# Value products on plain fp32 operands in the last slots of both expert layers

## The chip, the cores and the metric

One Trainium2 chip, one core. The metric is device time in microseconds (us) of one launch. The engines are TensorE (PE, with its weight loads shown as PEld), VectorE (DVE), ScalarE (ACT), GpSimd (POOL) and SyncE (SP), which here only issues transfers. The kernel before takes 2854.83 us, the median of 3 runs (2848.03 to 2857.15).

## The reference

Two trunk layers of a diffusion backbone over 384 tokens (128 context, 256 latent) of width 1024, each a mixer (attention with gated linear attention, then a state-space layer) and an expert layer called PEER. Only the expert layer is touched:

```
def peer_ffn(h, w_query, sub_keys, u_tab, v_tab):
    ...                       # 8 heads, top 16 of 128 x 128 product keys: idx, gates g
    def block(args):
        hx, ix, gx = args
        act = jax.nn.gelu(jnp.einsum('td,tkd->tk', hx, u_tab[ix]))
        return jnp.einsum('tk,tkd->td', gx * act, v_tab[ix])
```

Each of 384 tokens picks 128 of 16,384 experts. An expert is a row of u_tab, whose product with the token goes through gelu and a gate, and a row of v_tab, which is added with that weight. All data are fp32.

## The kernel before, in words

**Dense and fetched tokens.** Most tokens are computed densely, against all experts, in 128 blocks of 128 experts. The first tokens (64 in layer 0, 128 in layer 1) are instead served by fetching their own expert rows: POOL issues an indirect transfer of 128 rows of 4 KB (L2273) into a ring of 3 (layer 0) or 5 (layer 1) buffers, and DVE multiplies or adds one such tile (`fetched`, L2428 to L2449). That leaves 320 dense tokens in layer 0 and 256 in layer 1. Layer 0 has 64 fetched tokens and so 128 tiles, one a slot; layer 1 has 256 tiles, two a slot.

**Slots.** The dense part runs in a ring. A slot z.n (0 to 127) does the value products of block n and the score products of block n + RING, where RING is 36 in layer 0 and 38 in layer 1. In the last 36 slots of layer 0 (from 92) and the last 38 of layer 1 (from 90) there is no score block left; they hold value products alone.

**High and low parts.** A product of fp32 matrices is made of fp32r products: ACT copies a high part rounded to fp32r, DVE subtracts it to get the low part (`lo_part`, L163), and TensorE adds high x high, high x low and low x high.

**One slot without a score block**, engine by engine, each in program order:
- SP (L1966): waits until the low part of value block n is made (`vlow`), then loads value block n + VALUES (512 KB, L1928) into the buffer that block n frees. VALUES is 2 in layer 0 and 4 in layer 1. Behind it in the same queue it loads stored gates (L1932) once `applied` allows: in layer 0 the gates of slot n + 2 in every slot (160 KB), in layer 1 those of four slots in every fourth (384 KB). In layer 0 there follow now and then a modulation row of layer 1 (`mrow`, 512 KB, L1989) and a store of a state-space table (`s_wv`, 512 KB, L1769).
- DVE (L2547): `apply` multiplies the activations of slot n + 1 by their gates (L2489, and L2492 in layer 1); in layer 0 it then does one modulation operation (L2529, slots 6 to 117) and two table builds (L1792 to L1807, slots 8 to 103); then `value_low` and `gated_low`, the low parts of value block and gated activations of slot n + 1 (all at L163); then `fetched` once or twice.
- ACT (L2234): `value_high` (L2216) and `gated_high` (L2222) of slot n + 1.
- TensorE (L2084): waits `vlow` and `wlow`, then runs 16 fp32r matmuls with 512 moving columns in layer 0 (4 of them at L2091 for the folded tile of 64 tokens, 12 at L2097) and 12 in layer 1, and increments `valued`.

All of it is written as one fixed order per engine; only semaphores tie the engines together.

Of the kernel before, what the change touches and what calls it, by code (L numbers as in the profile page):

```python
# [32 lines left out]
P = 128  # L33
# [4 lines left out]
NT = T // P  # L38
# [59 lines left out]
class Stage:  # L98


    def __init__(self, nc, sems, name):
        self.nc, self.sems, self.name, self.mem = nc, sems, name, ExitStack()
# [1561 lines left out]
NB = NKEYS  # L1664
CT = 8
HALF = P // 2
# [17 lines left out]
class Plan:  # L1684
# [3 lines left out]

    def __init__(self, fetched, groups, held, each, values, early):
        self.fetched = self.first = fetched
        self.folded = fetched == HALF
        self.tokens = T - fetched
        self.tiles = range(fetched // P, NT)
        self.chunks, self.parts = self.tokens // CT, self.tokens // HALF
        self.held, self.each, self.values = held, each, values
        self.stored = self.parts - held
        self.odd_stored = (self.parts + 1) // 2 - held
        self.spans = [range(sum(groups[:g]), sum(groups[:g + 1])) for g in range(len(groups))]  # L1700
        assert self.spans[-1].stop == self.chunks
        self.last = GATED + len(groups)
        self.ring = self.last + TAIL
        self.fetches = [[] for _ in range(self.last + NB)]
        n = 2 * fetched
        for i in range(n):
            at = GATED + i * len(groups) // early if i < early else self.last + (i - early) * NB // (n - early)
            self.fetches[at].append(i)
# [3 lines left out]
        return (part + self.parts) % 2  # L1712


PLANS = Plan(64, [3] * 12 + [2] * 2, 0, 1, 2, 0), Plan(128, [2] * 16, 1, 4, 4, 0)


class Slot:
# [8 lines left out]

    def has(self, ahead):
        return self.n + ahead < NB

    def turn(self, ahead):
        return (self.n + ahead) // 2
# [110 lines left out]
def mix_experts(nc, s, cx, d, layer, plan, hi, lo, acc, total, ahead):  # L1843
# [75 lines left out]
    with nc.Block() as block:  # L1919
        @block.sync  # L1920
        def _(sp):
            def table(block, b):
                src = d["peer_u"][layer, bass.ds(block, 1)]
                sp.dma_start(ur[:, b], src.rearrange("a p (k m) -> p (a k) m", k=KC)).then_inc(uload[b], 16)

            def value(n):
                src = d["peer_v"][layer, bass.ds(n, 1)]
                sp.dma_start(loaded_value(n), src.rearrange("a p m -> p (a m)")).then_inc(vload[n % VALUES], 16)  # L1928

            def gate(m):  # L1930
                src = gates_dram[0:plan.stored, :, m * EACH:(m + 1) * EACH, :]
                sp.dma_start(gr[:, m % 2], src.rearrange("h p a c -> p h (a c)")).then_inc(gload[m % 2], 16)  # L1932

            sp.dma_start(keys[:], d["sub_keys"][layer]).then_inc(keys_loaded, 16)
            for b in range(2):
                sp.sem_inc(uload[b], 16)
            with sp.Fori(1, J // 2) as i:
                for b in range(2):
                    sp.wait_ge(ulow, i * 4 + 2 * b + 2)
                    src = d["w_query"][layer, bass.ds(i * 2 + b, 1)]  # L1940
                    sp.dma_start(ur[:, b], src.rearrange("a p k m -> p (a k) m")).then_inc(uload[b], 16)
            sp.wait_ge(nm.ready, KC)
            sp.dma_start(d["x_kept"], cx.x[:]).then_inc(xkept, 16)
            with sp.Fori(0, (LOW + 2) // 2) as i:
                for b in range(2):
                    sp.wait_ge(ulow, i * 4 + 2 * (J + b) + 2)
                    table(i * 2 + b, b)
            for n in range(LOW + 2, RING + 2):
                if n == RING - 2:
                    sp.wait_ge(gst0, 16 * PIECES * (PARTS // 2))  # L1950
                    value(0)
                    value(1)
                if n == RING:
                    sp.wait_ge(gst1, 16 * plan.odd_stored)
                    if plan.held:
                        sp.wait_ge(gst2, 16 * (PIECES - 1) * plan.odd_stored)
                    gate(0)
                    gate(1)
                sp.wait_ge(ulow2, n - 2 - LOW + 1)
                table(n, n % 2)  # L1960
            sp.wait_ge(gated, CHUNKS)
            for n in range(2, VALUES):
                value(n)
            sp.dma_start(cx.x[:], d["x_kept"]).then_inc(xback, 16)

            def slot(z):  # L1966
                b = z.n % 2
                if z.has(VALUES):
                    sp.wait_ge(vlow, z.n + 3)
                    value(z.n + VALUES)  # L1970
                if z.has(RING + 2):
                    sp.wait_ge(ulow2, z.n + (RING - LOW + 1))
                    table(z.n + (RING + 2), b)
                if z.has(2):
                    if (z.n + 1) % EACH == 0 and z.n + 1 + EACH < NB:
                        sp.wait_ge(applied, z.n + 1)
                        if z.n + 2 >= SOON and not plan.held:
                            sp.wait_ge(gst2, 16 * ((PIECES - 1) * (plan.odd_stored - 1) + 2))
                        gate((z.n + 1) // EACH + 1)
                if layer == 0:  # L1980
                    if z.n == ROWS_FROM - ROWS_AHEAD:
                        sp.wait_ge(gst2, 16 * ((PIECES - 1) * ((PARTS + 1) // 2 - 1) + 2))
                        sp.dma_start(silu[:], d["silu"]).then_inc(silu_loaded, 16)
                        sp.dma_start(bias[:], d["ada_b"].rearrange("p l j -> p (l j)")[:, 2 * MODS - LATE_MODS:]).then_inc(late_loaded, 16)
                        sp.dma_start(normg[:], d["norm_g"][:, 2:4]).then_inc(late_loaded, 16)
                    for row in (r for r in range(LATE_MODS) if row_slot(r) - ROWS_AHEAD == z.n):
                        if row >= ROWS_AHEAD:
                            sp.wait_ge(row_used, row - ROWS_AHEAD + 1)
                        sp.dma_start(mrow[:, row % ROWS_AHEAD], d["ada_rows"][IN_ROWS + OUT_ROWS + row]).then_inc(row_loaded[row % ROWS_AHEAD], 16)  # L1989
                    builds.transfers(sp, z.n)  # L1990

            for n in range(NB):
                slot(Slot(plan, n))
            sp.wait_ge(xback, 16)
            if layer == 0:
                sp.wait_ge(builds.stored, 16 * Builds.UNITS)

        @block.tensor
        def _(pe):
# [83 lines left out]

            def slot(z):  # L2084
                b = z.n % 2
                pe.wait_ge(vlow, z.n + 3)
                pe.wait_ge(wlow, z.n + 1)
                if plan.folded:
                    for rhs in (vh, vl):
                        for c in range(2):  # L2090
                            pe.matmul(acc[:, c, :], r32(pair[:, b, 0:P]), r32(rhs[:, b, c * 512:(c + 1) * 512]),  # L2091
                                      start=False, stop=False, skip_group_check=True)
                for t in range((FROM + HALF) // P, NT):
                    w = slice(t * P - FROM, (t + 1) * P - FROM)
                    for lhs, rhs in ((wh, vh), (wh, vl), (wl, vh)):
                        for c in range(2):
                            mm = pe.matmul(acc[:, 2 * t + c, :], r32(lhs[:, b, w]), r32(rhs[:, b, c * 512:(c + 1) * 512]),  # L2097
                                           start=False, stop=False, skip_group_check=True)
                mm.then_inc(valued, 1)
                if z.has(RING):  # L2100
                    product(z.n + (J + RING), b, ulow2, z.n + (RING - LOW + 1), whole=True)
# [5 lines left out]
        def _(act):  # L2107
# [126 lines left out]
            def slot(z):  # L2234
                b = z.n % 2
                if z.has(RING - 1):
                    if z.n:
                        act.wait_ge(wlow, z.n)
                    gelu(z.n + (J + RING - 1), 1 - b, z.place(-1))
                if z.has(1):  # L2240
                    value_high(z, 1)
                    gated_high(z, 1)
                if z.has(RING + 1):
                    high(z.n + (J + RING + 1), 1 - b, z.turn(J + RING + 1), uhigh2)
                expert_gelu(LAST + z.n)
                if z.n == 0 and not plan.held:
                    store_rest(PARTS - 1, SOON + REST, NKEYS)
# [29 lines left out]
        def _(dve):  # L2277
# [269 lines left out]
            def slot(z):  # L2547
                if z.has(1):
# [6 lines left out]
                            modulated()  # L2555
                    if layer == 0:
                        builds.operations(dve, z.n)
                    value_low(z, 1)
                    gated_low(z, 1)
                if z.has(RING + 1):  # L2560
                    table_low(z.n + (RING + 1), 1 - z.n % 2)

# [674 lines left out]
```

## Time and profile before

| | |
|---|---|
| median of 3 runs | 2854.83 us (2848.03 to 2857.15) |
| the profiled execution | 2854.96 us, its span 2853.2 us |
| PE busy | 2521.9 us (88%) |
| DVE busy | 2383.7 us (84%) |
| ACT busy | 1183.1 us (41%) |
| POOL busy | 682.9 us (24%) |
| DMA | 699.98 MB, mean 245 GB/s |
| mean granted TensorE clock | 0.947 of full |

The span runs from the first to the last instruction. Times in rows are us from its start. A matmul's row shows its whole latency, longer than the distance to the next one; so the rate is read from distances of starts, or from the busy time (a union) of a group over its count. In a row the last figures behind the bar are busy time and mean ns of one, and behind a second bar the idle time of the engine just before the group.

### The profile page before, as it was taken

What the parts mean: (1) busy time and instruction counts of PE and PEld (TensorE: products, weight loads), DVE (VectorE), ACT (ScalarE), POOL (GpSimd) and SP (SyncE); (2) the same over time, 40 slices, a digit from 0 to 9 for tenths busy, and PEclk for the clock granted to TensorE, in tenths of its full rate; (3) what the DMA queues carried; (4) which work ended last, traced back from release to release, by engine and by line L of the source; (5) the groups of instructions that cost most, each with busy time, mean ns of one, the idle gap of its engine ahead of it and who ended that gap; (6) DMA issues with size and microseconds to landing.
All of it is one profiled execution on the core that took longest, in us unless ns stands there. A gap on an engine that the chain in (4) does not pass through costs nothing. (4 is left out here: it accounts for less than half of the span.)

```text
span 2853.2 us, 44082 instructions
## 1 busy us (share of the span) xinstructions
PE 2521.9 (88%) x16181; PEld 2236.0 (78%) x16181; DVE 2383.7 (84%) x4754; ACT 1183.1 (41%) x1806; POOL 682.9 (24%) x486
## 2 busy tenths in 40 slices
PE   7986798789999999998788787998789999999765
PEld 3974698678999999997667776887779999999553
DVE  7877669986999999999985365469989999999997
ACT  3344344673333333333234322344574444444332
POOL 0000053001111111222320000035004555555662
PEclk9997799999999999999998898989899999999998
DMA  5720333469999999998972232224569999999994
GB/s 215 277 88 27 141 126 119 186 240 326 300 309 307 313 311 301 312 310 275 307 227 112 103 105 79 101 88 142 183 241 400 389 394 394 390 388 387 355 372 176
DMA packets 278137, 699.98 MB, mean 245 GB/s; under 512 B 105728, under 2 KB 120864, under 8 KB 271536
## 3 DMA queue, kind: packets, MB, share of 16 engines
q1 hardware_dynamic: 218112, 462.40, 47.2%
q0 software_dynamic: 55360, 201.38, 18.5%
q10 hardware_dynamic: 4464, 33.56, 2.9%
q8 instruction: 122, 2.00, 0.3%
q14 instruction: 79, 0.65, 0.1%
HBM read 636.69 MB, written 60.52 MB: 244 GB/s over the span
## 5 line engine op out<-in xcount | busy, mean ns | idle before, releaser
L2014 PE MATMUL pe_s<-hl_hi,pq_uh 128*128 128x320 f32 (+2 forms) x2304 | 711.4, 309 | 48.0 <-DVE pq_ul L163 21.0
L2015 PE MATMUL pe_s<-hl_lo,pq_uh 128*128 128x320 f32 (+2 forms) x2304 | 701.3, 304 | 0.0
L2016 PE MATMUL pe_s<-hl_hi,pq_ul 128*128 128x320 f32 (+2 forms) x2304 | 700.6, 304 | 0.0
L2097 PE MATMUL peer_acc<-val_vh,val_w 128*128 128x512 f32 x2048 | 602.9, 396 | 50.3 <-DVE val_w L163 50.3
L2014 PEld LDWEIGHTS pe_s<-hl_hi,pq_uh 128*128 128x128 f32 x2304 | 444.7, 193 | 71.8 <-issue 40.7
L2097 PEld LDWEIGHTS peer_acc<-val_vh,val_w 128*128 128x128 f32 x2048 | 381.1, 191 | 138.9 <-DVE val_vl L163 63.8
L2273 POOL DMA_INDIRECT pe_frow<-in_peer_rows,pe_fidx x192 | 258.7, 1347 | 838.2 <-DVE pe_frow L2433 780.2
L2015 PEld LDWEIGHTS pe_s<-hl_lo,pq_uh 128*128 128x128 f32 x2304 | 445.6, 193 | 8.5
L2016 PEld LDWEIGHTS pe_s<-hl_hi,pq_ul 128*128 128x128 f32 x2304 | 445.2, 193 | 0.0
L2131 ACT ACTIVATE pe_A<-pe_s 128x320 f32<-128x320 f32 (+1 forms) x256 | 105.9, 414 | 719.6 <-PE pe_s L2016 718.7
L2273 POOL DMA_INDIRECT pe_frow<-in_peer_v,pe_fidx x192 | 296.9, 1547 | 409.2 <-DVE pe_fh L2449 215.4
L2259 POOL TENSOR_TENSOR pq_ul<-pq_ur,pq_uh 128x512 fp32r<-128x512 f32 x96 | 125.8, 1331 | 843.6 <-ACT pq_uh L2115 843.4
L2097 PE MATMUL peer_acc<-val_vl,val_w 128*128 128x512 f32 x1024 | 320.2, 394 | 0.0
L163 DVE TENSOR_TENSOR pq_ul<-pq_ur,pq_uh 128x1024 fp32r<-128x1024 f32 x240 | 293.6, 1224 | 23.5 <-ACT pq_uh L2117 22.4
L163 DVE TENSOR_TENSOR val_vl<-val_vr,val_vh 128x1024 fp32r<-128x1024 f32 x192 | 234.8, 1223 | 54.5 <-ACT val_vh L2216 54.1
L2117 ACT ACTIVATE pq_uh<-pq_ur 128x1024 fp32r<-128x1024 f32 x236 | 248.1, 1051 | 37.9 <-DMA pq_ur<-in_peer_u 37.7
L2216 ACT ACTIVATE val_vh<-val_vr 128x1024 fp32r<-128x1024 f32 x192 | 202.4, 1054 | 92.9 <-DMA val_vr<-in_peer_v 70.5
L2433 DVE SCALAR_TENSOR_TENSOR pe_frow<-pe_frow,pe_fh 128x1024 f32<-128x1024 f32 x192 | 229.3, 1219 | 0.0
L2097 PEld LDWEIGHTS peer_acc<-val_vl,val_w 128*128 128x128 f32 x1024 | 195.0, 190 | 43.1
L2222 ACT ACTIVATE val_w<-pe_A 128x320 fp32r<-128x320 f32 (+1 forms) x256 | 112.5, 440 | 173.1 <-DVE pe_A L2492 138.0
L2151 ACT ACTIVATE gate_stg<-peer_acc 128x1024 f32<-128x1024 f32 x72 | 137.2, 2020 | 1.9 <-ACT gate_stg L2151 1.4
L163 DVE TENSOR_TENSOR val_w<-pe_A,val_w 128x256 fp32r<-128x256 f32 (+1 forms) x384 | 124.3, 351 | 5.9 <-ACT val_w L2222 5.9
(492 smaller groups left out, 4132.6 us busy)
## 6 DMA issues: line engine op xcount, KB each, us to landing
pq_ur<-in_peer_u SPq DMA_DIRECT2D x256, 512.0 KB, 5.9
val_vr<-in_peer_v SPq DMA_DIRECT2D x192, 512.0 KB, 5.4
val_more_vr<-in_peer_v SPq DMA_DIRECT2D x64, 512.0 KB, 6.7
gates<-gate_stg ACTq DMA_DIRECT2D x29, 1024.0 KB, 6.5
val_mrow<-in_ada_rows SPq DMA_DIRECT2D x56, 512.0 KB, 6.4
val_gr<-gates SPq DMA_DIRECT2D x128, 160.0 KB, 5.6
pq_ur<-in_w_query SPq DMA_DIRECT2D x32, 512.0 KB, 3.5
s_wv<-val_out SPq DMA_DIRECT2D x32, 512.0 KB, 7.4
```

The costliest lines, as they stand in the source:

```text
L163: return nc.vector.tensor_tensor(r32(out), x, hi, ALU.subtract)
L2014: pe.matmul(o, r32(uh[:, b, k]), r32(hi[:, k, a:T]), start=k == 0, stop=False)
L2015: pe.matmul(o, r32(uh[:, b, k]), r32(lo[:, k, a:T]), start=False, stop=False)
L2016: mm = pe.matmul(o, r32(ul[:, b, k]), r32(hi[:, k, a:T]), start=False, stop=k == KC - 1)
L2097: mm = pe.matmul(acc[:, 2 * t + c, :], r32(lhs[:, b, w]), r32(rhs[:, b, c * 512:(c + 1) * 512]), start=False, stop=False, skip_group_check ...
L2117: nc.scalar.activation(r32(uh[:, b]), ur[:, b], copy).then_inc(uhigh2, 1)
L2151: nc.scalar.activation(out, src, copy, scale=1.0 / GATE_SCALE).then_inc(evacd, 1)
L2216: nc.scalar.activation(r32(vh[:, b]), loaded_value(n), copy).then_inc(vhigh, 1)
L2222: nc.scalar.activation(r32(wh[:, b]), A[:, z.place(ahead)], copy).then_inc(whigh, 1)
L2259: nc.gpsimd.tensor_tensor(r32(ul[:, b, h]), ur[:, b, h], uh[:, b, h], ALU.subtract).then_inc(ulow, 1)
L2273: nc.gpsimd.indirect_dma_start(ft.rows[:, b], None, table.rearrange("l a b m -> (l a b) m"), bass.IndirectOffsetOnAxis(ft.index[:, k:k + 1 ...
L2433: v.scalar_tensor_tensor(row, row, 1.0, ft.h[:], ALU.mult, ALU.mult, accum_out=ft.act[:, k:k + 1]).then_inc(ft.used, 1)
```

## The change

A plan gets a first slot from which the value products are `whole`: 92 in layer 0, 90 in layer 1. In those slots ACT and DVE make no high and low parts; TensorE reads the loaded value block and the gated activations as they are, in plain fp32 matmuls; and SP reloads a value buffer when the products of its slot are done.

```
-    def __init__(self, fetched, groups, held, each, values, early):
+    def __init__(self, fetched, groups, held, each, values, whole, early):
...
+        self.whole_from = NB - self.ring if whole else NB
...
+    def whole(self, ahead=0):
+        return self.n + ahead >= self.plan.whole_from
... # SP
-                    sp.wait_ge(vlow, z.n + 3)
+                    sp.wait_ge(valued if z.whole() else vlow, z.n + 3)
                     value(z.n + VALUES)
... # TensorE, ahead of the old body of the slot
+                if z.whole():
+                    pe.wait_ge(vload[z.n % VALUES], z.n // VALUES * 16 + 16)
+                    pe.wait_ge(applied, z.n + 1)
+                    if plan.folded:
+                        for c in range(2):
+                            pe.matmul(acc[0:HALF, c, :], A[:, z.place(), 0:HALF], loaded_value(z.n)[:, c * 512:(c + 1) * 512],
+                                      start=False, stop=False, skip_group_check=True)
+                    for t in range((FROM + HALF) // P, NT):
+                        for c in range(2):
+                            mm = pe.matmul(acc[:, 2 * t + c, :], A[:, z.place(), t * P - FROM:(t + 1) * P - FROM],
+                                           loaded_value(z.n)[:, c * 512:(c + 1) * 512], start=False, stop=False, skip_group_check=True)
+                    mm.then_inc(valued, 1)
+                    return
... # ACT
-                if z.has(1):
+                if z.has(1) and not z.whole(1):
                     value_high(z, 1)
                     gated_high(z, 1)
... # DVE
-                    value_low(z, 1)
-                    gated_low(z, 1)
+                    if not z.whole(1):
+                        value_low(z, 1)
+                        gated_low(z, 1)
```

## Rows read from the trace of the kernel before

**Rows 1.** Windows: busy us of each engine, granted clock, DMA share, GB/s

```profile
core 0: us, PE busy (x) PEld busy (x) DVE busy (x) ACT busy (x) POOL busy (x), PEclk, DMA share, GB/s
717.00:1292.00 575.00, 575.00 (x3206) 522.50 (x3206) 541.93 (x858) 215.99 (x322) 100.67 (x80) 1.00 0.94 307
1310.00:1376.00 66.00, 50.37 (x214) 39.05 (x213) 64.27 (x105) 18.27 (x25) 19.42 (x11) 0.97 0.90 289
1381.00:1442.00 61.00, 52.27 (x208) 39.61 (x206) 56.04 (x90) 18.68 (x25) 17.26 (x13) 0.94 0.96 313
2300.00:2600.00 300.00, 300.00 (x1922) 273.90 (x1921) 287.57 (x449) 143.60 (x217) 162.30 (x107) 1.00 1.01 392
2650.00:2800.00 150.00, 105.13 (x398) 76.87 (x396) 141.01 (x200) 46.99 (x65) 96.64 (x66) 0.94 0.96 362
```

**Rows 2.** Line L2489 by windows: count, ns min/median/max, first and last start

```profile
L2489 DVE TENSOR_TENSOR pe_A<-pe_A,val_gr x13: 480/484/489, 1306.5 to 1375.9; 128x320 f32<-128x320 f32 x13
L2489 DVE TENSOR_TENSOR pe_A<-pe_A,val_gr x13: 480/485/494, 1381.6 to 1439.3; 128x320 f32<-128x320 f32 x13
L2489 DVE TENSOR_TENSOR pe_A<-pe_A,val_gr x10: 481/488/494, 1443.7 to 1481.2; 128x320 f32<-128x320 f32 x10
L2489 DVE TENSOR_TENSOR pe_A<-pe_A,val_gr x38: 343/351/354, 2643.9 to 2812.5; 128x192 f32<-128x192 f32 x38
```

**Rows 3.** Timeline of DVE, one slot of layer 1: start, us, what

```profile
2808.25 0.35 DVE L2489 TENSOR_TENSOR pe_A<-pe_A,val_gr 128x192 f32<-128x192 f32 x1
...
2808.65 1.22 DVE L163 TENSOR_TENSOR val_vl<-val_more_vr,val_vh 128x1024 fp32r<-128x1024 f32 x1
...
2810.12 1.28 DVE L2449 SCALAR_TENSOR_TENSOR pe_fh<-pe_frow,pe_fw,pe_fh 128x1024 f32<-128x1024 f32 x1
...
2812.51 0.35 DVE L2489 TENSOR_TENSOR pe_A<-pe_A,val_gr 128x192 f32<-128x192 f32 x1
```

**Rows 4.** Timeline of DVE, one slot of layer 0

```profile
1359.15 0.48 DVE L2489 TENSOR_TENSOR pe_A<-pe_A,val_gr 128x320 f32<-128x320 f32 x1
...
1362.03 1.22 DVE L163 TENSOR_TENSOR val_vl<-val_vr,val_vh 128x1024 fp32r<-128x1024 f32 x1
...
1363.63 1.28 DVE L2449 SCALAR_TENSOR_TENSOR pe_fh<-pe_frow,pe_fw,pe_fh 128x1024 f32<-128x1024 f32 x1
...
1364.83 0.48 DVE L2489 TENSOR_TENSOR pe_A<-pe_A,val_gr 128x320 f32<-128x320 f32 x1
```

**Rows 5.** Groups on PE: the whole span, 30:36, and 1505:1508.5; plain fp32

```profile
L221 PE MATMUL mod_acc<-mod_w,mod_sg 128*2 128x512 f32 x64 | 30.2, 630 | 11.9 <-DMA mod_w<-in_ada_w 11.9
...
L221 PE MATMUL mod_acc<-mod_w,mod_sg 128*2 128x512 f32 x15 | 6.6, 592 | 0.0
...
L598 PE MATMUL in_ss<-l_zz,g_ones 128*128 128x384 f32 x11 | 3.7, 486 | 0.0
```

**Rows 6.** Timeline of PE: starts of slots 92, 124, 125; last matmuls of layer 0

```profile
1315.26 0.62 PE L2091 MATMUL peer_acc<-val_vh,val_w 128*128 128x512 f32 x2
...
1468.91 0.62 PE L2091 MATMUL peer_acc<-val_vh,val_w 128*128 128x512 f32 x2
...
1472.54 0.62 PE L2091 MATMUL peer_acc<-val_vh,val_w 128*128 128x512 f32 x2
...
1487.13 0.61 PE L2097 MATMUL peer_acc<-val_vh,val_w 128*128 128x512 f32 x2
```

**Rows 7.** Timeline of SP: the two loads of one slot of layer 0

```profile
1467.80 0.33 SPq L1928 DMA_DIRECT2D val_vr<-in_peer_v  x1
...
1468.23 0.38 SPq L1932 DMA_DIRECT2D val_gr<-gates  x1
```

**Rows 8.** Tile val_gr in 1304:1490 and in 2644:2820: issue to landing

```profile
DMA to landing us min/median/max: 3.6/5.3/8.8
...
DMA to landing us min/median/max: 6.0/7.7/10.9
```

**Rows 9.** SP's own waits, 1304:1490: us in total, times, longest

```profile
SPq L1928 <- DVE val_vl L163: 135.2, 35, 6.2
```

More of the change, by code:

```diff
@@ L1712, in half @@
         return (part + self.parts) % 2
-PLANS = Plan(64, [3] * 12 + [2] * 2, 0, 1, 2, 0), Plan(128, [2] * 16, 1, 4, 4, 0)
+PLANS = Plan(64, [3] * 12 + [2] * 2, 0, 1, 2, True, 0), Plan(128, [2] * 16, 1, 4, 4, True, 0)
 class Slot:
```

## The prediction, blind

> **What bounds the kernel now.** I begin with the windows [rows 1], since the change acts in two stretches only: slots 92 to 127 of layer 0 (about 1306 to 1488 us) and slots 90 to 127 of layer 1 (about 2644 to 2820 us). Ahead of each, TensorE is busy without a gap (575.00 of 575.00 us, 300.00 of 300.00). In the stretches it is not: 50.37 of 66 us, 52.27 of 61, 105.13 of 150. There DVE is the busy engine: 64.27 of 66, 56.04 of 61, 141.01 of 150. The DMA is nearly full too, a share of 0.90 and 0.96 in layer 0 and 0.96 in layer 1.
>
> The length of a slot follows from the starts of `apply` [rows 2]: (1375.9 - 1306.5) / 12 = 5.8 us in slots 92 to 104, with table builds; (1439.3 - 1381.6) / 12 = 4.8 in 105 to 117; (1481.2 - 1443.7) / 9 = 4.2 in 118 to 127; and (2812.5 - 2643.9) / 37 = 4.56 in layer 1. An undisturbed slot is DVE's own chain without a gap: 2812.51 - 2808.25 = 4.26 us in layer 1 [rows 3], 1364.83 - 1359.15 = 5.68 in layer 0 [rows 4]. So today DVE sets the slot, and transfers that land late add 0.3 us to the mean.
>
> **What goes.** On DVE a slot loses the two low parts: from 2808.65 to 2810.12, 1.47 us, in layer 1 [rows 3]; from 1362.03 to 1363.63, 1.60 us, in layer 0 [rows 4]. DVE alone would then want 5.68 - 1.60 = 4.1 us a slot in layer 0, and less from slot 105 on, where the builds end, and 118 on, where the modulation ends; in layer 1 it would want 4.26 - 1.47 = 2.8. ACT loses its two copies; it is off the path (18.27 of 66 us busy), so this is worth nothing.
>
> **What comes: the matmuls.** A plain fp32 matmul is in this trace two MATMUL instructions: L221 is called 32 times (4 tiles by 8 chunks) and stands x64 [rows 5]. Fifteen of them with 512 columns keep PE busy 6.6 us at an own latency of 0.592, so their distance is (6.6 - 0.17) / 15 = 0.429 us [rows 5]. That row has only 2 stationary columns; with 128 and 384 moving ones it is (3.7 - 0.17) / 11 = 0.321, which is 0.429 x 384 / 512: the stationary side adds nothing. One fp32 matmul thus costs 0.858 us. The fp32r ones: 16 in 1472.54 - 1468.91 = 3.63 us, 0.227 each [rows 6], three for one product 0.68. Plain fp32 is dearer on TensorE, and more so for the folded tile, which had two and not three.
> - Layer 0: 6 matmuls, 12 x 0.429 = 5.15 us a slot instead of 3.63.
> - Layer 1: 4 matmuls, 8 x 0.429 = 3.43 us instead of 12 x 0.227 = 2.72.
>
> **What moves: the reload.** SP waits for `valued` instead of `vlow`. `value_low` of slot n runs in DVE's slot n - 1, so before, the reload left ahead of slot n's products; now it leaves after they end, and the gates of slot n + 2, the modulation rows and the table stores stand behind it in the same queue. SP already spends 135.2 us of the stretch waiting there [rows 9]; it will wait longer. In layer 0, with two value buffers, this closes a loop: products n end, +0.05 SP wakes, +0.43 the gate load is issued behind the value load [rows 7], +Lg it lands, +0.55 `apply` (0.485) and its semaphore, +0.05 products n + 2 begin and take 5.4 (12 x 0.429, the last one's latency 0.17 longer, a start after idleness 0.1). Two slots take 1.1 + Lg + 5.4, one slot (6.5 + Lg) / 2, and never under 5.15. Lg was 3.6 at least, 5.3 in the median and 8.8 at most [rows 8]. DVE has time left in such a slot (it wants 4.1 or less), so it waits at `apply` when the gates land.
>
> With Lg 5.3 a slot takes 5.9 us. I take that for slots 94 to 104, whose traffic and length stay as they were. In the 23 slots behind, a slot gets longer with the same bytes or fewer, and so the DMA emptier; I take Lg 4.5, the middle between the least and the median, and 5.5 us.
>
> The Trainium skill, DMA: Bandwidth & Descriptors, Anatomy of one DMA, fits a transfer at about 2.0 us plus bytes over 436 GB/s. By it the 672 KB of value block and gates land in about 3.6 us, an estimate that equals the least landing of [rows 8]; the loop would then hide behind the matmuls, which is rival A below. The median row says otherwise for a loaded queue.
>
> **The sum, layer 0.** Products 92 start at 1315.26 behind the last score block [rows 6], as before, and end at 1320.6. Slot 93 has its data: 1325.8. Then 11 x 5.9 = 64.9 and 23 x 5.5 = 126.5 us: the last products end at 1517.2. Before they ended at 1487.13 + 0.61 = 1487.7, and the next block began with them. **+29.5 us.** Bounds: matmuls alone 1320.6 + 35 x 5.15 = 1500.9, +13; Lg 5.3 in all 34 slots 1526.4, +39.
>
> **The sum, layer 1.** Neither DVE (2.8) nor TensorE (3.43) fills 4.56 us. Four value buffers leave three slots, some 13 us, for a reload, and the gates of slots n + 5 on still more, against landings of at most 10.9 [rows 8]; no loop closes. What is left is the DMA: 362 GB/s at a share of 0.96 over 150 us, 54.3 MB [rows 1]. Scaled to the share 1.01 of the layer's body that is 362 x 1.01 / 0.96 = 381 GB/s. So 54.3 MB take 142.5 us: -7.5. I take **-6 us**, since the last slots run empty. Bounds: 0, if the waits for landing rows just grow, and -12 at the body's 392 GB/s (54.3 / 0.392 = 138.5).
>
> The same page, Where 436 GB/s comes from, names some 358 GB/s as one core's share of HBM. By it this stretch is full already and layer 1 gives nothing, which would make the sum about 2884. The body's 392 over 300 us disagrees, and the trace decides.
>
> Together +23.5 on the profiled execution's 2854.96, which is 0.1 above the median: **2878 us**.
>
> **Rivals.**
> - A, short landings (0.15): the gates land in 4 us or less once DVE and the queues are lighter, and TensorE alone sets layer 0 at 5.15 to 5.2. For it: 3.6 occurs. Against: the median at a similar load. +13 to +15, with layer 1 2861 to 2864.
> - B, the other side (0.06): layer 1 isn't held by the DMA but falls to TensorE's 3.5 us a slot, 37 x (4.56 - 3.5) = -39, against +29.5: 2845, faster. It decides from 3.76 us a slot, 29.5 / 37 below 4.56; with A already from 4.2. Against: 54.3 MB / 150 x 4.56 is 1.65 MB a slot, and 3.5 us would need 471 GB/s, where 392 is the most held.
> - C, long landings (0.09): value block, gates and fetched rows now leave in one bunch after each slot; with Lg 6.5 a slot takes 6.5, the end is at 1325.8 + 34 x 6.5 = 1546.8, +59, layer 1 zero: 2914.
> - D, fp32 is not what the rows say for this shape (0.03): at the fp32r distance an instruction, a slot has 2.7 us of matmuls, the loop takes 4.6, layer 0 loses nothing in sum and layer 1's 6 us remain: 2849.
>
> **How the numbers follow.** The forecast has 0.67, from 2866 to 2892. A measurement tells 0.3%, 8.6 us, from no change. Faster (under 2846): two thirds of B and a little of D, 0.06. Same (up to 2863): most of A, the rest of B and D, 0.13. Slower 0.81. The range reaches from A, 2861, to the upper bound of layer 0 with layer 1 at zero, 2893; outside are B, C and D.
>
> **What would show it.** The changed trace should have plain fp32 MATMULs at 0.43 us distance, x12 a slot in layer 0 and x8 in layer 1; `apply` at 5.9 and then 5.5 us in layer 0, idle ahead of it because of `val_gr`; SP waiting on the products; layer 1 at 4.4 us with DVE at some two thirds and the DMA at 0.98 to 1.0; granted clock 1.0 in both. The forecast is wrong if layer 0 keeps under 5.2 us a slot, if its idle time before the products is not ended by the gates' chain, or if layer 1 falls below 4.2.

## The result, and the profile after

| | before | changed |
|---|---|---|
| median, same chips (6 runs each) | 2857.0 us (2848.03 to 2860.46) | 2879.82 us (2877.6 to 2884.48) |
| ratio, 95% interval | | 1.0086 (1.007 to 1.0101): slower, by less than 1% |
| the profiled execution, its span | 2854.96, 2853.2 us | 2877.6, 2875.7 us |
| mean granted TensorE clock | 0.947 | 0.953 |

The total came out within 2 us of the forecast, though neither layer did: each lies beyond its own bound, on opposite sides. To see that, measure each stretch from its own start: from `apply` of the first slot without a score block to `ad_fold`, the first DVE operation of the block behind the expert layer. Its row before:

```profile
L2606 DVE TENSOR_TENSOR ad_fold<-g_const x2: 225/226/226, 1488.1 to 2821.1; 128x64 f32<-128x64 f32 x2
```

With the starts of [rows 2] that is 1488.1 - 1306.5 = 181.6 us in layer 0 and 2821.1 - 2643.9 = 177.2 in layer 1. After, `apply` (now L2506) by windows and `ad_fold`:

```profile
L2506 DVE TENSOR_TENSOR pe_A<-pe_A,val_gr x13: 485/493/494, 1309.7 to 1391.5; 128x320 f32<-128x320 f32 x13
L2506 DVE TENSOR_TENSOR pe_A<-pe_A,val_gr x12: 491/493/494, 1396.9 to 1462.2; 128x320 f32<-128x320 f32 x12
L2506 DVE TENSOR_TENSOR pe_A<-pe_A,val_gr x10: 491/493/494, 1473.5 to 1522.5; 128x320 f32<-128x320 f32 x10
L2506 DVE TENSOR_TENSOR pe_A<-pe_A,val_gr x39: 351/351/359, 2680.8 to 2835.4; 128x192 f32<-128x192 f32 x39
L2624 DVE TENSOR_TENSOR ad_fold<-g_const x2: 226/226/226, 1530.8 to 2843.7; 128x64 f32<-128x64 f32 x2
```

Layer 0 takes 1530.8 - 1309.7 = 221.1 us, **39.5 more** (forecast 29.5, its upper bound 39). Layer 1 starts its stretch at 2686.4 (the second start of its row) and takes 157.3, **19.9 less** (forecast 6, its bound 12). That is 19.6; the other 3 us of the 22.6 between the two profiled executions stand ahead of the first stretch, where the code is the same.

The windows [rows 1] after, moved with the stretch in layer 1:

```profile
core 0: us, PE busy (x) PEld busy (x) DVE busy (x) ACT busy (x) POOL busy (x), PEclk, DMA share, GB/s
717.00:1292.00 575.00, 575.00 (x3204) 522.44 (x3203) 541.74 (x858) 216.61 (x325) 100.76 (x80) 1.00 0.93 307
1310.00:1376.00 66.00, 60.78 (x164) 25.75 (x164) 39.56 (x61) 0.88 (x2) 10.54 (x10) 1.00 0.72 228
1381.00:1442.00 61.00, 55.92 (x123) 19.11 (x121) 32.76 (x47) 0.00 (x0) 9.40 (x10) 1.00 0.83 262
2300.00:2600.00 300.00, 300.00 (x1927) 274.14 (x1926) 288.38 (x464) 140.58 (x216) 168.63 (x107) 1.00 1.01 393
2680.00:2830.00 150.00, 136.88 (x354) 61.62 (x353) 110.67 (x152) 3.48 (x6) 74.95 (x74) 1.00 1.02 403
```

In layer 0 DVE and ACT are relieved as meant (64.27 to 39.56 of 66 us; 18.27 to 0.88), TensorE is the busy engine, and yet nothing is full: the DMA fell from 0.90 to 0.72. That is what a loop of waits looks like. In layer 1 the DMA rose from 362 to 403 GB/s. The clock stays at its upper level of 2.4 GHz in both.

The timeline of one slot of layer 0 shows the loop, and answers to [rows 4, 6, 7]:

```profile
1404.96 1.90 PE L2095 MATMUL peer_acc<-val_vr,pe_A 128*64 128x512 f32 x4 [1.82 <-DVE pe_A L2506]
1406.80 3.70 PE L2099 MATMUL peer_acc<-val_vr,pe_A 128*128 128x512 f32 x8
1410.53 0.33 SPq L1932 DMA_DIRECT2D val_vr<-in_peer_v  x1
1410.54 1.90 PE L2095 MATMUL peer_acc<-val_vr,pe_A 128*64 128x512 f32 x4
1410.95 0.39 SPq L1936 DMA_DIRECT2D val_gr<-gates  x1
1414.87 0.49 DVE L2506 TENSOR_TENSOR pe_A<-pe_A,val_gr 128x320 f32<-128x320 f32 x1 [2.14 <-DMA val_gr<-gates]
1416.00 1.93 PE L2095 MATMUL peer_acc<-val_vr,pe_A 128*64 128x512 f32 x4
```

Products end at 1410.50; SP reloads at 1410.53; the gates leave at 1410.95; `apply` starts 3.9 us later. Four MATMULs of the folded tile and eight of the two full tiles are the twelve forecast, but from 1410.54 to 1416.00 they fill 5.46 us, not 5.15. The waits of DVE and PE (1310 to 1520 us) and of SP (1304 to 1515) answer to [rows 9]; columns: total us, times, longest:

```profile
DVE pe_A L2506 <- DMA val_gr<-gates: 103.6, 33, 11.8
...
PE peer_acc L2095 <- DVE pe_A L2506: 13.1, 17, 1.8
```

```profile
SPq L1932 <- PE peer_acc L2099: 167.1, 33, 16.1
```

DVE waits for gates in 33 slots, and TensorE then waits for DVE in 17 of them, 13.1 us. That half of the slots show no wait doesn't mean that TensorE set them: the loop runs over two slots, and the products of slot n + 1 run while the reload of slot n is under way. Only late in the layer does TensorE go without such a wait for long, in the eight slots that start from 1474.31 to 1512.84 us; there its products alone set the slot.

The landing times [rows 8] stand in no view of this trace, but since DVE was idle before every `apply`, the time from the gates' issue (L1936) to `apply` gives them: mean 5.6 us in slots 94 to 104, 5.1 in 105 to 117, 4.1 in 118 to 127 (lowest 3.56, highest 6.77 of 34). The slots took (1391.48 - 1329.66) / 10 = 6.2, (1468.21 - 1391.48) / 13 = 5.9 and (1522.55 - 1468.21) / 10 = 5.4 us.

### The profile page after: what moved, and what is told of

Same layout as the page of the kernel before. It is cut to its first block and busy times, and to the rows that moved or that the text cites. A ratio compares the mean times of both kernels' runs of the same rounds, so it can differ in the third digit from the quotient of the medians.

```text
span 2875.7 us, 43010 instructions
## 1 busy us (share of the span) xinstructions
PE 2596.6 (90%) x15885; PEld 2166.4 (75%) x15885; DVE 2276.6 (79%) x4570; ACT 1073.6 (37%) x1658; POOL 629.4 (22%) x486
## 5 line engine op out<-in xcount | busy, mean ns | idle before, releaser
L2018 PE MATMUL pe_s<-hl_hi,pq_uh 128*128 128x320 f32 (+2 forms) x2304 | 713.0, 309 | 45.1 <-DVE pq_ul L163 22.6
L2114 PE MATMUL peer_acc<-val_vh,val_w 128*128 128x512 f32 x1456 | 422.0, 391 | 0.0
L2290 POOL DMA_INDIRECT pe_frow<-in_peer_v,pe_fidx x192 | 247.7, 1290 | 472.5 <-DVE pe_fh L2466 234.1
L2114 PEld LDWEIGHTS peer_acc<-val_vh,val_w 128*128 128x128 f32 x1456 | 267.4, 188 | 51.5 <-issue 0.2
L2114 PE MATMUL peer_acc<-val_vl,val_w 128*128 128x512 f32 x728 | 224.7, 390 | 0.0
L163 DVE TENSOR_TENSOR val_vl<-val_vr,val_vh 128x1024 fp32r<-128x1024 f32 x138 | 169.1, 1225 | 49.8 <-ACT val_vh L2233 48.1
L2099 PE MATMUL peer_acc<-val_vr,pe_A 128*128 128x512 f32 x432 | 198.8, 604 | 10.7 <-DVE pe_A L2509 10.5
L2506 DVE TENSOR_TENSOR pe_A<-pe_A,val_gr 128x320 f32<-128x320 f32 (+1 forms) x256 | 107.7, 421 | 123.1 <-DMA val_gr<-gates 123.1
L2099 PEld LDWEIGHTS peer_acc<-val_vr,pe_A 128*128 128x128 f32 x432 | 77.9, 189 | 130.8 <-issue 129.1
L2114 PEld LDWEIGHTS peer_acc<-val_vl,val_w 128*128 128x128 f32 x728 | 137.0, 188 | 29.9
L2233 ACT ACTIVATE val_vh<-val_vr 128x1024 fp32r<-128x1024 f32 x138 | 145.3, 1053 | 5.9 <-DMA val_vr<-in_peer_v 5.9
```

Source lines behind the costliest of these rows:

```text
L163: return nc.vector.tensor_tensor(r32(out), x, hi, ALU.subtract)
L2018: pe.matmul(o, r32(uh[:, b, k]), r32(hi[:, k, a:T]), start=k == 0, stop=False)
L2099: mm = pe.matmul(acc[:, 2 * t + c, :], A[:, z.place(), t * P - FROM:(t + 1) * P - FROM], loaded_value(z.n)[:, c * 512:(c + 1) * 512], star ...
L2233: nc.scalar.activation(r32(vh[:, b]), loaded_value(n), copy).then_inc(vhigh, 1)
L2290: nc.gpsimd.indirect_dma_start(ft.rows[:, b], None, table.rearrange("l a b m -> (l a b) m"), bass.IndirectOffsetOnAxis(ft.index[:, k:k + 1 ...
L2506: ins = v.tensor_tensor(a, a, gr[:, m % 2, :, at:at + HALF], ALU.mult)
```

## The experiments

Times of the kernel before are from the same chips: 2855.67 us with the first four runs told here (e1 to e4), 2855.15 with e5 to e8, 2854.22 with e9 to e11. "Stretch" is the measure above. A stretch is read from one trace each. Layer 0 without the change took 180.3 to 182.1 us in four traces (before, e1, e7, e11); with it, 221.1 in the changed kernel and 227.1 in e2. So where the loop is at work a stretch repeats to some 6 us only, and there the medians weigh more.

### One layer at a time (e1, e2)

```
-PLANS = Plan(64, ..., 0, 1, 2, True, 0), Plan(128, ..., 1, 4, 4, True, 0)
+PLANS = Plan(64, ..., 0, 1, 2, False, 0), Plan(128, ..., 1, 4, 4, True, 0)   # e1
+PLANS = Plan(64, ..., 0, 1, 2, True, 0), Plan(128, ..., 1, 4, 4, False, 0)   # e2
```

> The change in layer 1 alone (its last 38 slots); layer 0 keeps high and low parts. My theory: the two traces say layer 1 gained some 20 us (last value product 42.5 us late at its slot 90, 22.8 us late at its end) by letting the DMA run full, and that gain stands by itself: 2835 to 2840 us, 0.6% to 0.7% faster than before, slots of 4.0 to 4.1 us, DMA at 400 GB/s. Rival (my prediction's own term): layer 1 is worth 6 us, and the rest of the 20 is the drift of one profiled execution: 2849 to 2853 us.

> The change in layer 0 alone (its last 36 slots). My theory: the loss there is some 39 us by the traces, more than the 29.5 that I gave it: 2892 to 2898 us, slots of 6.0 to 6.1 us. Rival: the term was right at 29.5 and the trace was a slow one: 2884 to 2887 us. With the run on layer 1 alone the two should add up to the whole change, +23 us, if they don't touch each other.

e1: 2834.05 us, ratio 0.9922 (0.9908 to 0.9935), stretches 182.1 and 157.9. e2: 2899.55 us, 1.0146 (1.0125 to 1.0167), stretches 227.1 and 177.2. So layer 1 gains 21.6 us and layer 0 loses 43.9; together 22.3, against 22.8 for the whole change. By these medians the layers don't touch each other, and the good total of the forecast was two errors of opposite sign. The loss of 39.5 that the changed trace shows is at the low end: that execution, 2877.6 us, was the fastest of its six.

### Is it the loop? Gates first (e3), deeper buffers (e4)

e3 sends the gates of slot n + 2 ahead of the value reload, so they no longer wait for the products:

```
+                gates_first = layer == 0 and z.whole()
+                if gates_first and z.has(2):
+                    sp.wait_ge(applied, z.n + 1)
+                    gate(z.n + 2)
                 if z.has(VALUES):
                     sp.wait_ge(valued if z.whole() else vlow, z.n + 3)
```

e4 gives layer 0 four value buffers from slot 94 on (the two table buffers `ur` are free by then), so a reload waits for products two slots older:

```
+            k = (n - DEEP) % 4
+            return ur[:, k].rearrange("p k m -> p (k m)") if k < 2 else vr[:, k - 2]
...
+                            sp.wait_ge(valued, z.n + 1)     # before: z.n + 3
```

> The whole change, but in layer 0's last 36 slots SP issues the gate load ahead of its wait for the products, so that only the value block is left in the loop. Theory 1 (the loop runs through gates and apply): a two-slot turn loses the 0.43 us of the second issue, the apply of 0.5 us and the gates' own landing; slot about (0.05 + 5.2 + 0.05 + 5.5) / 2 = 5.4 us instead of 6.1: some 20 us back, 2858 to 2865. Theory 2 (the loop runs through the value block as much as through the gates, its landing being as long): at most 0.5 us a slot, 5.7 or more, 2865 to 2875. Theory 3 (TensorE's matmuls alone set the slot): no change, 2880.

> The whole change, but in layer 0's last slots the value blocks go round four buffers instead of two (the two raw score buffers are free there), so that SP waits for the products of slot n - 2 and not n before it loads block n + 2 and gates n + 2. If the reload loop is what made layer 0 6.1 us a slot, only the matmuls are left: 12 x 0.429 = 5.15 to 5.25 us a slot, layer 0 costs 15 to 18 us and not 39, and the whole lies at 2852 to 2860 us. If the matmuls with their waits cost 6 us whatever the buffers, it stays at 2880. Idle time of TensorE in the stretch should go from 12 of 205 us to near nothing only in the first case.

e3: 2871.1 us, 1.0052 (1.0036 to 1.0067), stretch 213.4. e4: 2864.54 us, 1.0034 (1.0021 to 1.0048), stretch 206.9. The windows of e3 and of e4:

```profile
1310.00:1376.00 66.00, 61.67 (x171) 26.68 (x170) 42.04 (x64) 0.88 (x2) 11.12 (x11) 1.00 0.76 238
```

```profile
1310.00:1376.00 66.00, 66.00 (x164) 25.57 (x163) 48.67 (x73) 0.44 (x1) 11.49 (x13) 1.00 0.91 301
```

In e3 the wait goes over to the value block; this is who waits there:

```profile
PEld peer_acc L2099 <- DMA val_vr<-in_peer_v: 16.3, 13, 3.1
```

The loop is real, and closes through either transfer of the reload. With four buffers TensorE has no gap left (66.00 of 66) and the loop is gone; but the stretch is still 206.9 and the slot 5.5 us (the distance of TensorE's starts below), where twelve MATMULs at 0.429 us make 5.15. Something inside TensorE costs the rest.

### What is in a TensorE slot (e5, e8)

Both edits start from e4. e5 takes 128 stationary columns for the folded tile too (the upper 64 rows get products of other tokens that are not wanted there); e8 puts the second 512 columns into the upper 64 rows, which the kernel adds to the lower ones anyhow:

```
-                            pe.matmul(acc[0:HALF, c, :], A[:, z.place(), 0:HALF], ...
+                            pe.matmul(acc[:, c, :], A[:, z.place(), 0:P], ...                          # e5
+                            pe.matmul(acc[c * HALF:(c + 1) * HALF, c, :], A[:, z.place(), 0:HALF], ... # e8
```

> The kernel with four value buffers, but the folded tile's matmuls take 128 stationary columns and write 128 rows instead of 64 (the upper 64 rows so get products of other tokens added). In the four-buffer run TensorE was never idle, 190 of 190 us, and yet a slot took 5.49 us and not 12 x 0.429 = 5.15: starts are 0.52 us apart where the stationary tile changes between 64 and 128 columns, and 0.48 to 0.53 behind it. Theory: the change of tile size costs 0.17 us each time, two in a slot; here it is gone: 5.15 to 5.2 us a slot, 11 to 12 us less than with four buffers, 2852 to 2854. Rival: the 0.3 us is the slot's waits (semaphores at its start), and stays: 2864.

> Four value buffers, and the folded tile's two fp32 products go to different halves of the array: columns 0 to 511 into rows 0 to 63, columns 512 to 1023 into rows 64 to 127 of its accumulator, which are added at the end anyway. Theory: matmuls on different column halves run side by side (as the two halves of the folded tokens' transposes do in the trace), so that the folded tile costs 2 x 0.429 and not 4: (8 + 2) x 0.429 + 0.34 = 4.63 us of TensorE a slot against 5.49: layer 0's stretch 31 us shorter than with four buffers if TensorE stays the bound, 2833; a few us more if the DMA (0.91 busy at 301 GB/s in slots 92 to 104) fills: 2830 to 2840, as good as the change in layer 1 alone. Rival: they don't overlap in fp32: 2864.

e5: 2853.4 us, 0.9993 (0.9982 to 1.0005), stretch 194.6. e8: 2834.12 us, 0.9928 (0.9913 to 0.9943), stretch 176.3. PE's timelines of e4, e5 and e8 (start, us; L2112 is the folded tile, L2116 the full ones):

```profile
1440.83 1.93 PE L2112 MATMUL peer_acc<-pq_ur,pe_A 128*64 128x512 f32 x4
1442.70 3.70 PE L2116 MATMUL peer_acc<-pq_ur,pe_A 128*128 128x512 f32 x8
1446.33 1.07 PE L2112 MATMUL peer_acc<-val_vr,pe_A 128*64 128x512 f32 x2
```

```profile
1441.45 1.88 PE L2112 MATMUL peer_acc<-val_vr,pe_A 128*128 128x512 f32 x4
1443.16 3.60 PE L2116 MATMUL peer_acc<-val_vr,pe_A 128*128 128x512 f32 x8
1446.60 0.59 PE L2112 MATMUL peer_acc<-val_vr,pe_A 128*128 128x512 f32 x1
```

```profile
1439.63 1.08 PE L2112 MATMUL peer_acc<-pq_ur,pe_A 128*64 128x512 f32 x4
1440.64 3.70 PE L2116 MATMUL peer_acc<-pq_ur,pe_A 128*128 128x512 f32 x8
1444.27 1.08 PE L2112 MATMUL peer_acc<-pq_ur,pe_A 128*64 128x512 f32 x4
```

From one L2112 to the next: 5.50 us in e4, 5.15 in e5, 4.64 in e8. With one width, 12 x 0.429 comes out exactly. With 64 columns beside 128 there is 0.17 us more at each of the two changes a slot: four small ones take 1.87 instead of 1.72, eight large ones 3.63 instead of 3.43. In e8 the same four take 1.01 us: the two column halves run side by side. Against e4 that is 30 us for one index. e10, told below, takes away one of the two changes of width a slot: from one pair of full tiles to the next, two slots are 1446.83 - 1437.90 = 8.93 us, 4.46 a slot and 0.17 less than in e8, as expected.

```profile
1437.90 7.13 PE L2119 MATMUL peer_acc<-pq_ur,pe_A 128*128 128x512 f32 x16
1446.83 7.13 PE L2119 MATMUL peer_acc<-val_vr,pe_A 128*128 128x512 f32 x16
```

The Trainium skill, TensorEngine Tiling (Array Packing), Key Properties, says both: a change of the tiling mode drains the engine, and different tiles can run matmuls in parallel. By these runs the trace agrees, with 0.17 us a change, and nearly half of the pair's time saved. That the 0.17 us is the page's drain is our reading; the runs show what a change costs, not what happens in it.

### The reload alone (e6)

The kernel before, its parts kept, with only SP's wait moved in the last 36 slots of layer 0:

```
+                    late_wait = layer == 0 and z.n + RING >= NB
+                    sp.wait_ge(valued if late_wait else vlow, z.n + 3)
```

> The kernel before, with one line of the change in layer 0's last 36 slots: SP waits for the products (valued) and not for the low part (vlow) before it reloads. High and low parts and fp32r matmuls stay. Theory (the reload loop is the dear part): products end, +0.05, value block lands 5.2, high part 1.06, low part 1.22, low part of the gates 0.56, waits 0.2, products 3.8: 12.1 us for two slots, 6.0 us a slot against 5.0: +35, 2885 to 2895, as slow as the whole change in layer 0 though no fp32 matmul is in it. Rival (the fp32 matmuls are the dear part): the DVE-bound slots of 5.7 hide the reload, 2855 to 2868.

2944.29 us, 1.0307 (1.0284 to 1.0329), stretch 275.0: +89, the largest effect of the study, and far more than expected. The windows and a piece of the timeline:

```profile
1310.00:1376.00 66.00, 45.96 (x184) 36.12 (x182) 49.51 (x80) 14.25 (x20) 9.54 (x9) 0.89 0.67 208
1381.00:1442.00 61.00, 38.67 (x127) 29.42 (x126) 39.59 (x62) 12.23 (x16) 8.77 (x8) 0.78 0.66 209
1442.00:1560.00 118.00, 76.79 (x254) 59.57 (x254) 62.83 (x104) 23.76 (x31) 20.02 (x15) 0.79 0.58 183
```

```profile
1418.98 1.06 ACT L2217 ACTIVATE val_vh<-val_vr 128x1024 fp32r<-128x1024 f32 x1 [9.79 <-DMA val_vr<-in_peer_v]
...
1423.85 1.19 PE L2092 MATMUL peer_acc<-val_vh,val_w 128*128 128x512 f32 x2 [6.47 <-DVE val_w L163]
...
1429.94 0.64 PE L2098 MATMUL peer_acc<-val_vh,val_w 128*128 128x512 f32 x2
...
1430.61 0.33 SPq L1928 DMA_DIRECT2D val_vr<-in_peer_v  x1
...
1434.28 0.33 SPq L1928 DMA_DIRECT2D val_vr<-in_peer_v  x1
...
1435.58 1.06 ACT L2217 ACTIVATE val_vh<-val_vr 128x1024 fp32r<-128x1024 f32 x1 [9.62 <-DMA val_vr<-in_peer_v]
```

Here the chain has the landing, ACT's copy, two DVE operations and the products one behind the other, and the slots go in pairs. TensorE waits 6.47 us before the pair shown, and from 1310 to 1580 us 92.0 us in 21 such waits, the longest 7.2:

```profile
PE peer_acc L2092 <- DVE val_w L163: 92.0, 21, 7.2
```

After the wait its granted clock is at the lower level of 1.2 GHz for a while (the two matmuls of L2092 take 1.19 us, those of [rows 6] 0.62), which makes the chain longer again: the fourteen matmuls from 1423.85 to 1429.94 take 6.09 us, where 14 x 0.227 would be 3.18. So the lower clock cost this pair some 2.9 us, an estimate from these rows. On average two slots took 15.1 us, 2 x 7.55 by the starts of `apply`, against the 12.1 expected. So the late reload is by itself the bad part of the change in layer 0, and with the parts dropped it costs less: 89 alone, 44 with fp32 products in place of the parts. e6 has the longer chain and the lower clock at once; how much of its 89 is the clock was not separated over the whole stretch.

### Is layer 1 held by the DMA? (e7)

e1 with half of each value block loaded from slot 94 of layer 1 on; the other half of the buffer keeps old data:

```
+                if layer == 1 and n >= plan.whole_from + VALUES:
+                    sp.dma_start(loaded_value(n)[:, 0:D // 2], src[:, 0:D // 2])...
```

> The change in layer 1 alone, and from slot 94 on only the first 512 of 1024 columns of each value block are loaded (the others keep what was there); fetches, gates, DVE and TensorE do as much as before. Theory (layer 1's last slots are held by the DMA at some 402 GB/s): 1.65 MB a slot become 1.39, 3.46 us, so that TensorE's 8 x 0.429 = 3.43 and its start share the bound: 3.5 to 3.6 us a slot, 15 us less than with layer 1 alone, 2817 to 2822. Rival (the ring of five fetch buffers, latency and not bandwidth, sets 4.03 us): the slot stays over 3.9 and the time at 2830 to 2834.

2825.09 us, 0.9892 (0.9874 to 0.9911), stretch 147.1, slot 3.74 instead of 4.03:

```profile
2650.00:2785.00 135.00, 130.18 (x301) 56.01 (x300) 105.46 (x145) 0.38 (x1) 87.63 (x73) 0.99 0.98 369
```

Fewer bytes are faster, so the transfers did hold the stretch, and TensorE's 3.43 us come next (130.18 of 135 us busy). The gain is less than expected, a slot of 3.74 us and not 3.5 to 3.6: the DMA is still just as full, 0.98, at 369 GB/s only. That the shorter rows (2 KB of each 4) are the reason is likely but not shown, and whether it was their bytes or their landing times that held the slot was not separated. The lesson for the forecast stands either way: the share of the DMA engines' time doesn't say how many bytes more there are to be had.

### Better versions (e9, e10), and e1 again (e11)

e9 keeps the parts in layer 0 (and plain fp32 in layer 1), and loads its value blocks into four buffers three slots ahead. e10 is e8 with the folded products behind the full ones in odd slots, so that a width changes once a slot and not twice.

```
+                            if n < DEEP + 2:                      # e9, on SP
+                                sp.wait_ge(scored, n - 4 + J + RING + 3)
+                            else:
+                                sp.wait_ge(vlow, n - 4 + 3)
+                            value(n)
...
+                    if plan.folded and b == 0:                    # e10, on TensorE
+                        fold_products()
+                        mm = full_products()
+                    elif plan.folded:
+                        full_products()
+                        mm = fold_products()
```

> Layer 1 whole as in the change; layer 0 keeps high and low parts, but its value blocks go round four buffers and are loaded three slots ahead. Theory: in layer 0 before, the slots from 105 on were 0.4 to 0.9 us longer than DVE's own chain (4.4, then TensorE's 3.63) because ACT waited for the value block to land; with the block early, they come near 4.5 and 3.8, 6 to 9 us less than with layer 1 alone: 2825 to 2829. Rival: there the DMA is full (0.96 to 0.99 busy), and an earlier request only waits longer: 2832 to 2836, the same.

> The kernel with four value buffers and the folded tile in two halves, and in every odd slot of layer 0's last 36 the folded products come behind the full ones, so that the size of the stationary tile changes once a slot and not twice. Theory: 0.17 us less of TensorE a slot, 4.46 and not 4.63: 6 us less, 2826 to 2830, if TensorE is the bound. Rival: the DMA, at 0.96 to 0.97 in those slots, is it already: 2832 to 2835, the same.

> The change in layer 1 alone once more, on the same chip and beside the two others, as what they are compared with: 2831 to 2837 us, 0.7% to 0.8% faster than before. No theory expects anything else.

e9: 2826.07 us, 0.9905 (0.9888 to 0.9922), stretch of layer 0 172.2. e10: 2828.09, 0.9912 (0.9896 to 0.9928), 170.2. e11: 2836.7, 0.9937 (0.9923 to 0.9951), 180.3. Both beat the kernel before and the change of layer 1 alone (the slowest run of either, 2832.66, is below e11's fastest, 2833.71); between e9 and e10 the intervals don't decide. ACT's waits in layer 0, of e1 (1304 to 1490 us) and e9 (1304 to 1480), show what e9 took away:

```profile
ACT val_vh L2233 <- DMA val_vr<-in_peer_v: 58.6, 22, 4.5
```

```profile
ACT val_vh L2252 <- PE peer_acc L2130: 69.9, 34, 2.2
```

With parts and two buffers, late value blocks held the chain in 22 slots; with four none does. DVE is then busy without a gap (61.00 of 61 us, 56.04 in the same window of [rows 1]), and the DMA is full beside it (the second window of e9, then of e10):

```profile
1381.00:1442.00 61.00, 53.34 (x220) 40.00 (x219) 61.00 (x98) 21.49 (x28) 23.69 (x14) 1.00 1.00 335
```

```profile
1381.00:1442.00 61.00, 61.00 (x166) 23.50 (x165) 37.94 (x57) 0.00 (x0) 13.44 (x14) 1.00 0.98 331
```

## Why the prediction was right in sum and wrong in its terms

- **What bounds the kernel before: half right.** "DVE sets the slot, and transfers that land late add 0.3 us to the mean" holds in slots 92 to 104: 5.78 us before, in e11 and in e9 alike. In slots 105 to 117 and 118 to 127 e9, which leaves DVE its whole work and only loads earlier, has 4.45 and 3.77 us, against 4.88 and 4.19 before (distances of the starts of `apply`). So late value blocks cost some 0.4 us a slot there, more than the 0.3 that was read from layer 1 [rows 3], and the stretch is 8 us shorter than e11's (172.2 against 180.3).
- **The loop in layer 0: right.** SP waits 167.1 us for products, `apply` waits for gates, the DMA empties, and e3 and e4 take 9 and 15 us off. Rival A is out: the landings had a mean of 5.0 us, not 4 or less. Its "+13, matmuls alone" is what e5 reaches, 194.6 - 181.6 = +13.0, where both the loop and the changes of width are gone.
- **Its size: 39.5 in the changed trace and 43.9 by the medians of e2, not 29.5.** The formula holds. With the measured landings and 5.49 + 0.27 = 5.76 us for the products (the prediction's 5.15 and the same additions for latency and start), (1.1 + 5.0 + 5.76) / 2 = 5.93 us against 5.85 measured over slots 94 to 127. In e2 the same reading gives a mean landing of 5.2 us and so 6.0, against 6.06 measured; its longer landings account for the greater loss there. The mis-sized term is the product time of a slot, 5.15: it is 5.49 (e4), for the two changes of width that "the stationary side adds nothing" [rows 5] did not see, as both of those rows have one width only. That is 0.34 / 2 x 34 = 6 us of the 10. The landings, taken as 5.3 and 4.5 and measured as 5.6, then 5.1 and 4.1 (mean 5.0 against 4.8), are some 4 us. At the end of the layer TensorE's 5.49 was the floor, where the prediction had 5.15. The experiments split the loss another way: e5 - before = 13.0 us for the matmuls alone, e4 - e5 = 12.3 for the changes of width, changed - e4 = 14.2 for the loop. The prediction had 13, nothing and 16.5: what it lacked is the middle term.
- **Layer 1: the mechanism right, the size wrong.** DMA-bound was right (e7), and rival B is out: the slot fell to 4.03 us, not to 3.5. It is below the 4.2 that was named as a sign against the forecast, so by its own sign the forecast of this layer was wrong. The mis-sized term is the DMA's capacity: 362 GB/s scaled by the share, 1.01 / 0.96, gave 381; it carried 403. 177.2 x 362 / 403 is 159.2 us, and 157.3 was measured. Even the bound, the body's 392, was beaten: the share rose 6%, the bytes per us 11%. What let the same engines carry more at nearly the same share was not tested.
- **The sum is right by luck.** Layer 0 was 10 to 14 us worse than forecast and layer 1 some 14 to 16 better, and nothing in the prediction ties the one error to the other.
- **The Trainium skill's two rules.** The Trainium skill, DMA: Bandwidth & Descriptors, Anatomy of one DMA, gave 3.6 us for value block and gates; it is a fit for transfers that GpSimd issues, and these are issued by SP, which the prediction doesn't say. The lowest issue-to-`apply` time here is 3.56 but the mean 5.0, and no run here has an empty queue to hold the rule against. The Trainium skill's section Where 436 GB/s comes from, on the same page, puts a core's share of HBM at some 358 GB/s, and has a measured 425 beside it; as a bound for one core at work alone the trace disagrees with the 358, with 403 over 150 us.
- **The folded tile.** The prediction counted its fp32 matmuls as dear and stopped there. e8 shows that they needn't be: side by side, they make layer 0 faster (176.3) than before (181.6) even in plain fp32.

## What to carry to other kernels

Cut work from the busy engine only after asking what releases its buffers: here the same edit moved a reload from before the products to behind them, and with two buffers that closed a loop of landing plus products over two slots; four buffers open it. Forecast each stretch by itself and report each, since a good total may be two errors. A DMA share of 0.96 is no measure of what room is left: read GB/s against the most that the same transfers have carried, and leave the bound open above it.

## What the hardware showed beyond expectation

- A change between 64 and 128 stationary columns costs TensorE 0.17 us (e4 against e5, and e8 against e10).
- Plain fp32 matmuls on the two column halves overlap: four MATMULs in 1.01 us where one after the other took 1.87 (e8 against e4).
- The DMA held 403 GB/s for 150 us in layer 1, above the 393 of the layer's body; with rows of 2 KB in place of 4 KB it was as full at 369.
- With waits of up to 7.2 us on TensorE its mean granted clock was 0.78 (e6, 1381 to 1442 us); with gaps of at most 1.8 us it was 1.00 (the changed kernel).
